# Scratch of the placed expert weights: from key pair, partition, token tile to partition, token tile, key pair

## The chip, the cores and the metric

One core of a Trainium2 chip runs the whole kernel. The metric is the device time of one execution in microseconds.

## What is computed

The kernel is one layer of a hybrid backbone for 1024 latent and 256 context tokens (10 tiles of 128, width 1024): modulated norm, an input projection, neighbourhood and context attention, a bidirectional gated scan, an output projection, and then PEER, a product-key layer of experts with one neuron each. The change is in PEER:

```
s = einsum('nhpd,pkd->nhpk', q, sub_keys)            # 8 heads, two halves, 128 keys
...                                                  # top 16 of each, top 16 of their sums
expert = (idx1 * N_KEYS + idx2)                      # 128 of 16384 experts for each token
g = softmax(best)                                    # a weight for each of them
act = gelu(einsum('cd,ced->ce', x_c, u[e_c]))
out = einsum('ce,ced->cd', g_c * act, v[e_c])
```

## The kernel before

Six of the ten token tiles fetch the rows of u and v that their tokens chose, with indirect DMAs that GpSimd issues. The first four tiles (512 tokens, "dense") go through all 16384 experts instead: 64 rounds of one key pair, 2 x 128 experts. A round computes gelu of the products of the tokens with u (two u tiles, `exp_a_ps`, L2573), multiplies it by the placed weights (L2838), which are 0 where a token did not choose the expert, and multiplies by v (`exp_o_ps`, L2600 and L2605). In the same rounds gathered tiles are worked off beside it: rounds 0 to 7 ("keys") fetch 10 or 14 key rows each, the later ones 8 key rows and two groups of four value rows, each row 128 x 4 KB.

**The placing stage** (`place_weights`) makes the placed weights of the dense tiles. For each tile there are 8 steps of 16 tokens, in four batches of 4 tokens. VectorE makes one-hots (L2110 to L2125), ScalarE scales them or makes a part of them (L2215 to L2229), TensorE multiplies them, and ScalarE copies the products into the grid (`placed`, L2237). There are two grids, tile t writes grid t % 2, so tile 2 waits at its first copy for the store of tile 0, tile 3 for that of tile 1. A grid holds 64 KB in each partition, in the order key pair r, token half h, key of the pair e, token n (for the last tile: half first). Partition a is the second key. Beside it, GpSimd fetches 24 key rows and the last 56 value rows of a context tile, in a ring of six rows, four rows a group; TensorE takes a group (`late_products`, L2151) in the middle of every second step, in program order, and GpSimd refills the rows only when the group is done.

The stores go to a scratch tensor in HBM. Sync issues tiles 0 to 2 whole (L2261) as each is placed, then the first half of tile 3's tokens (L2263), then of the second half the first two key pairs (L2265), while ScalarE's queue stores the other 62 pairs (L2253). Sync then waits for the stores of tiles 0 to 2, and the stage ends.

**The experts' stage** (`experts`). Sync's queue issues in each round the load of that round's placed weights into `g_raw` (L2488, after both products at L2838 of the round before), the v pair and two u tiles; in the late rounds in the order g, v (after TensorE's products of the round before), u, u (each after the u products that free it). VectorE needs `g_raw` at L2838. The load of round r, in the layout before, reads `scratch["g"][r]`, which is contiguous:

```
ROOM = {... "g": (N_KEYS // 2, P, DENSE_TILES, 2, 2, P // 2), ...}            # L2957
sp.dma_start(tile_target(t), tile_grid(t)).then_inc(stored[t % 2], 16)        # L2261
sp.dma_start(g_raw[:, :, :, :], scratch["g"][r].rearrange("a t h e n -> a (t h) e n"))  # L2488
```

So a store of a tile writes 128 x 64 runs of 1 KB (512 B for the halves of tile 3), and a load reads 128 runs of 4 KB.

Of the kernel before, what the change touches and what calls it, by code (L numbers as in the profile page):

```python
# [17 lines left out]
P = 128  # L18
D = 1024
KD = D // P  # L20
LATENT, CONTEXT = 1024, 256
T = LATENT + CONTEXT
TILES = T // P
LATENT_TILES = LATENT // P
DENSE_TILES = 4
# [12 lines left out]
N_KEYS = 128  # L38
# [1936 lines left out]
def place_weights(nc, io, keep, scratch, routes, ahead, edge):  # L1975
# [13 lines left out]
    with Scope(nc, "place") as s:  # L1989
# [35 lines left out]
        LAST_TILE = DENSE_TILES - 1  # L2025
        HALF_TOKENS = P // 2

        def tile_target(t):
            return scratch["g"].rearrange("r a t h e n -> a r t (h e n)")[:, :, t, :]

        def tile_grid(t):
            return grid[t % 2][:, :].rearrange("p (r x) -> p r x", x=2 * P)

        def half_target(h, lo, hi):
            return scratch["g"].rearrange("r a t h e n -> a r t h (e n)")[:, lo:hi, LAST_TILE, h, :]

        def half_grid(h, lo, hi):
            return grid[LAST_TILE % 2][:, :].rearrange("p (h r x) -> p h r x", h=2, x=P)[:, h, lo:hi, :]
# [137 lines left out]
        def _(act):  # L2176
# [64 lines left out]
            def body(t, m, before):  # L2241
# [9 lines left out]
            copy_batches(TOTAL - 1, (2, 3))  # L2251
            act.wait_ge(placed, DENSE_TILES * PER_TILE)
            nc.scalar.dma_start(half_target(1, FIRST_PAIRS, N_KEYS // 2), half_grid(1, FIRST_PAIRS, N_KEYS // 2))\  # L2253
              .then_inc(edge.g_rest, 16)

        @block.sync
        def _(sp):
            sp.dma_start(ahead.x[:, 0, :], scratch["h2"][0]).then_inc(edge.x_in[0], 16)
            for t in range(LAST_TILE):
                sp.wait_ge(placed, (t + 1) * PER_TILE)  # L2260
                sp.dma_start(tile_target(t), tile_grid(t)).then_inc(stored[t % 2], 16)  # L2261
            sp.wait_ge(placed, LAST_TILE * PER_TILE + PER_TILE // 2)
            sp.dma_start(half_target(0, 0, N_KEYS // 2), half_grid(0, 0, N_KEYS // 2)).then_inc(edge.g_half, 16)  # L2263
            sp.wait_ge(placed, DENSE_TILES * PER_TILE)
            sp.dma_start(half_target(1, 0, FIRST_PAIRS), half_grid(1, 0, FIRST_PAIRS)).then_inc(edge.g_first, 16)  # L2265
            sp.wait_ge(stored[0], 32)
            sp.wait_ge(stored[1], 16)


def experts(nc, io, keep, scratch, ahead, edge):  # L2270
# [21 lines left out]
    with Scope(nc, "exp") as s:  # L2292
# [13 lines left out]
        g_raw = s.sb("g_raw", [P, 2 * DENSE_TILES, 2, P // 2])  # L2306
        acc = keep["acc"]
        h2T = acc[:, :, :].rearrange("p t n -> p (t n)").rearrange("p (k n) -> p k n", k=KD)
# [35 lines left out]
        g_in = s.sem("g_in")  # L2344
# [36 lines left out]
        y_out = s.sem("y_out")  # L2381
        own_pool = s.sem("own_pool")
        block = s.block()
        v_pairs = io["v_rows"].rearrange("p (r e) n -> p r e n", e=PAIR)

        def f32(a):
# [43 lines left out]
        def at_least(r, n):  # L2430
            return not isinstance(r, int) or r >= n
# [37 lines left out]
        def _(sp):  # L2469
            def load_u(n, e):  # L2470
                if not has_key(n):
                    return
                sp.wait_ge(a_made, n + 1)
                sp.dma_start(u_in_lo[:, e, :, :], io["uT"][n]).then_inc(u_in[e], 16)

            def body(r, parity, mode, tile, _):
                if mode == "end":
                    load_rows()
                    return
                if tile == 0:  # L2480
                    sp.dma_start(xs[1], scratch["h2"][1]).then_inc(x_in[1], 16)
                def load_g():
                    if at_least(r, 1):
                        sp.wait_ge(weighted, 2 * r)
                    else:
                        sp.wait_ge(edge.g_half, 16)
                        sp.wait_ge(edge.g_first, 16)
                    sp.dma_start(g_raw[:, :, :, :], scratch["g"][r].rearrange("a t h e n -> a (t h) e n")).then_inc(g_in, 16)  # L2488

                if mode == "keys":  # L2490
                    if at_least(r, 1):
                        load_g()
                    load_u(2 * r + 2, 0)
                    load_u(2 * r + 3, 1)
                    if not at_least(r, 1):
                        load_g()
                    if at_least(r, 2):
                        sp.wait_ge(o_made, DENSE_TILES * (r - 1))
                    sp.dma_start(v_whole[parity][:, :, :], v_pairs[:, r, :, :]).then_inc(whole_in[parity], 16)
                else:  # L2500
                    load_g()
                    sp.wait_ge(o_made, DENSE_TILES * (r - 1))
                    sp.dma_start(v_raw[parity][:, :, :], v_pairs[:, r, :, :]).then_inc(v_in, 16)
                    for e in range(PAIR):
                        load_u(2 * r + 2 + e, e)
                if isinstance(r, int) and r == 1:
                    sp.wait_ge(edge.g_rest, 16)
                if tile is not None and tile >= 2:
                    store(tile - 2)
                if mode == "both" and tile is not None and tile + 1 < LATENT_GATHER:  # L2510
                    sp.wait_ge(dots, SLOTS * tile + RING)
                    sp.dma_start(xs[(tile + 1) % 2], scratch["h2"][tile + 1]).then_inc(x_in[(tile + 1) % 2], 16)

            def store(k):
                sp.wait_ge(out_ready, k + 2)
                sp.dma_start(scratch["ffn"][k + DENSE_TILES], out[:, :]).then_inc(out_stored, 16)

            def load_rows():
                sp.wait_ge(out_stored, 16 * LATENT_GATHER)
                sp.wait_ge(a_made, N_KEYS + 2)  # L2520
                sp.dma_start(gate_row[LATENT_COND], scratch["gate"][:, LATENT_COND, :]).then_inc(gate_in[LATENT_COND], 16)
                for t in STORED_TILES:
                    if t == STORED_TILES[-1]:
                        sp.wait_ge(dots, SLOTS * LATENT_GATHER + HALF_SLOTS + RING)
                    if t == LATENT_TILES:
                        sp.dma_start(gate_row[CONTEXT_COND], scratch["gate"][:, CONTEXT_COND, :])\
                          .then_inc(gate_in[CONTEXT_COND], 16)
                    sp.dma_start(ffn_row(t), scratch["ffn"][t]).then_inc(final_in[t], 16)
                    sp.dma_start(mixed_row(t), scratch["x1"][t]).then_inc(final_in[t], 16)
                    if t == STORED_TILES[0]:  # L2530
                        sp.dma_start(norm_w, io["norm_f"].partition_broadcast(P)).then_inc(norm_in, 16)
                for t in [SUMMED_TILE] + list(range(DENSE_TILES)):
                    sp.dma_start(mixed_row(t), scratch["x1"][t]).then_inc(final_in[t], 16)
# [420 lines left out]
            walk(dve, lambda r, parity, mode, tile, local: end(r) if mode == "end" else body(r, parity, mode, tile, local))  # L2954


ROOM = {"x1": (TILES, P, D), "h2T": (P, KD, DENSE_TILES * P), "g": (N_KEYS // 2, P, DENSE_TILES, 2, 2, P // 2),  # L2957
        "h2": (GATHER_TILES - CONTEXT_GATHER, P, D), "gate": (P, 2, D), "ffn": (TILES, P, D)}


def program(nc, io):
    scratch = {name: nc.dram_tensor(f"scratch_{name}", shape, FP32).ap() for name, shape in ROOM.items()}
    with Scope(nc, "keep") as s:
# [129 lines left out]
```

## Time and profile before

| what | value |
|---|---|
| median of 3 runs | 3399.52 us (3398.56 to 3399.75) |
| the profiled execution | 3391.75 us |
| its span, first to last instruction | 3389.2 us |
| TensorE, VectorE, GpSimd, ScalarE busy | 91%, 79%, 59%, 31% of the span |
| DMA | 1131.17 MB in 365083 packets, mean 334 GB/s |
| of it the gathers' queue (q0) | 221184 packets, 805.40 MB |
| of it Sync's queue (q1) | 135248 packets, 316.40 MB |
| of it ScalarE's queue (q10) | 8496 packets, 7.44 MB |
| placing stage, first to last copy into a grid | 1412.2 to 1613.7 us |
| rounds, first and last load at L2488 | 1635.4 and 3301.7 us |

Times in the trace count from the start of the span. A busy share is an average over stages; which wait comes last in a stage is read from windows, waits and timelines of that stage. In the counts of a queue every descriptor's move is a packet, and each gathered row adds a few packets of 4 bytes (the signals). The share of a queue is the time that its packets took over that of all 16 engines; packets overlap a little, so shares can add up to more than 100%.

### The profile page before, as it was taken

What the parts mean: (1) busy time and instruction counts of PE and PEld (TensorE: products, weight loads), DVE (VectorE), ACT (ScalarE), POOL (GpSimd) and SP (SyncE); (2) the same over time, 40 slices, a digit from 0 to 9 for tenths busy, and PEclk for the clock granted to TensorE, in tenths of its full rate; (3) what the DMA queues carried; (4) which work ended last, traced back from release to release, by engine and by line L of the source; (5) the groups of instructions that cost most, each with busy time, mean ns of one, the idle gap of its engine ahead of it and who ended that gap; (6) DMA issues with size and microseconds to landing.
All of it is one profiled execution on the core that took longest, in us unless ns stands there. A gap on an engine that the chain in (4) does not pass through costs nothing.

```text
span 3389.2 us, 46100 instructions
## 1 busy us (share of the span) xinstructions
PE 3081.4 (91%) x15031; PEld 2028.2 (60%) x15031; DVE 2663.5 (79%) x5959; ACT 1052.9 (31%) x1893; POOL 1983.3 (59%) x1674
## 2 busy tenths in 40 slices
PE   6879899789899998677699999999999999999996
PEld 4647344566455445366455677766777766677674
DVE  2327899688487999799699778887888888787888
ACT  4731244366111111488211222222222222222222
POOL 0000477444445555553588777787777777777771
PEclk9989999899899999899799999999999999999998
DMA  9422698665867888899999999999999999999997
GB/s 332 178 103 105 214 312 296 205 199 181 336 248 254 292 288 304 315 347 384 353 384 405 407 413 412 413 413 412 412 414 413 413 412 413 413 414 413 412 412 306
DMA packets 365083, 1131.17 MB, mean 334 GB/s; under 512 B 31944, under 2 KB 98760, under 8 KB 356608
## 3 DMA queue, kind: packets, MB, share of 16 engines
q0 software_dynamic: 221184, 805.40, 62.3%
q1 hardware_dynamic: 135248, 316.40, 24.5%
q10 hardware_dynamic: 8496, 7.44, 0.7%
q8 instruction: 80, 1.31, 0.1%
q14 instruction: 75, 0.61, 0.0%
HBM read 1075.93 MB, written 53.19 MB: 333 GB/s over the span
## 4 chain that ended last, share of the span: by engine, by line
PE 18%; DMA 12%; POOL 10%; issue 8%; DVE 3%; ACT 0%; POOLq 0%; SPq 0%; DVEq 0%; ACTq 0%
DMA exp_value_row<-in_v_rows,exp_v_id 11%; PE exp_a_ps L2573 8%; PE exp_o_ps L2600 5%; POOL exp_value_row L2729 5%; PE exp_v_ps L2557 3%; PE exp_o_ps L2605 2%; POOL edge_u_raw L2718 1%; POOL exp_more_row L2718 1%; POOL edge_row L2718 1%; POOL exp_value_row L2718 1%; DVE edge_u_raw L2783 1%; DMA exp_value_row<-in_u_rows,edge_id_and_dot 0%; DMA exp_final_row<-scratch_x 0%; DVE exp_u_lo L2747 0%; POOL exp_v_id L2700 0%
## 5 line engine op out<-in xcount | busy, mean ns | idle before, releaser
L423 POOL DMA_INDIRECT ahead_row<-in_u_rows,keep_tables x194 | 272.5, 1404 | 571.5 <-POOLq L102 356.3
L2729 POOL DMA_INDIRECT exp_value_row<-in_v_rows,exp_v_id x448 | 500.4, 1117 | 158.8 <-issue 134.7
L2573 PE MATMUL exp_a_ps<-exp_xT_hi,exp_u_hi 128*128 128x512 f32 x1024 | 410.8, 401 | 31.3 <-DVE exp_u_lo L2747 23.0
L2573 PE MATMUL exp_a_ps<-exp_xT_lo,exp_u_hi 128*128 128x512 f32 x1024 | 401.2, 392 | 0.0
L2573 PE MATMUL exp_a_ps<-exp_xT_hi,exp_u_lo 128*128 128x512 f32 x1024 | 400.5, 391 | 0.0
L2718 POOL DMA_INDIRECT edge_row<-in_u_rows,edge_id_and_dot x224 | 307.3, 1372 | 104.0 <-issue 48.4
L2656 ACT ACTIVATE exp_hidden<-exp_a_ps 128x512 f32<-128x512 f32 x128 | 76.6, 598 | 916.0 <-PE exp_a_ps L2573 916.0
L2864 DVE TENSOR_TENSOR keep_acc<-exp_o_ps,keep_acc 128x1024 f32<-128x1024 f32 x250 | 305.2, 1221 | 58.8 <-PE exp_o_ps L2600 52.5
L2600 PE MATMUL exp_o_ps<-exp_v_hi,exp_w_hi 128*128 128x512 f32 x896 | 287.3, 402 | 7.4 <-DVE keep_acc L2913 7.4
L2600 PE MATMUL exp_o_ps<-exp_v_lo,exp_w_hi 128*128 128x512 f32 x896 | 282.4, 396 | 0.0
L2600 PE MATMUL exp_o_ps<-exp_v_hi,exp_w_lo 128*128 128x512 f32 x896 | 280.5, 394 | 0.0
L2573 PEld LDWEIGHTS exp_a_ps<-exp_xT_hi,exp_u_hi 128*128 128x128 f32 x1024 | 193.3, 189 | 118.9 <-issue 48.0
L432 DVE CUSTOM_DVE_ANT_0 ahead_row<-ahead_row,ahead_x 128x1024 f32<-128x1024 f32 x194 | 231.0, 1219 | 25.8 <-DMA ahead_row<-in_u_rows,keep_tables 25.4
L2557 PE MATMUL exp_v_ps<-exp_value_row,exp_hot 128*32 128x512 f32 x1792 | 218.6, 600 | 29.1 <-DMA exp_value_row<-in_v_rows,exp_v_id 29.1
L1546 PE MATMUL queries_q_ps<-mix_featT,queries_slab 128*128 128x512 f32 (+1 forms) x640 | 230.3, 512 | 0.0
L495 POOL DMA_INDIRECT val_row<-in_v_rows,keep_tables x136 | 145.5, 1070 | 126.1 <-PE route_lat_h_ps L509 65.6
L2573 PEld LDWEIGHTS exp_a_ps<-exp_xT_hi,exp_u_lo 128*128 128x128 f32 x1024 | 193.3, 189 | 41.8
L2600 PEld LDWEIGHTS exp_o_ps<-exp_v_hi,exp_w_hi 128*128 128x128 f32 x896 | 164.3, 189 | 90.0 <-issue 45.3
L2573 PEld LDWEIGHTS exp_a_ps<-exp_xT_lo,exp_u_hi 128*128 128x128 f32 x1024 | 193.5, 189 | 39.9 <-issue 1.7
L2783 DVE CUSTOM_DVE_ANT_0 edge_row<-edge_row,keep_tables 128x1024 f32<-128x1024 f32 x128 | 155.9, 1218 | 56.3 <-DMA edge_row<-in_u_rows,edge_id_and_dot 56.3
L737 PE MATMUL proj_lat_ps<-mix_featT,heads_early_room 128*128 128x512 f32 x448 | 196.4, 596 | 1.8 <-ACTq L796 1.8
L2626 ACT ACTIVATE exp_u_hi<-exp_u_raw 128x1024 fp32r<-128x1024 f32 x126 | 132.6, 1053 | 195.9 <-DMA exp_u_raw<-in_uT 195.8
(451 smaller groups left out, 6375.4 us busy)
## 6 DMA issues: line engine op xcount, KB each, us to landing
exp_u_raw<-in_uT SPq DMA_DIRECT2D x126, 512.0 KB, 6.7
exp_v_raw<-in_v_rows SPq DMA_DIRECT2D x56, 1024.0 KB, 7.8
exp_g_raw<-scratch_g SPq DMA_DIRECT2D x64, 512.0 KB, 7.9
scratch_g<-place_grid SPq DMA_DIRECT2D x3, 8192.0 KB, 52.1
proj_ctx_mod_slab<-in_w_mod SPq DMA_DIRECT2D x8, 2048.0 KB, 13.3
heads_early_room<-in_w_in SPq DMA_DIRECT2D x10, 1024.0 KB, 12.5
mod_slab<-in_w_mod SPq DMA_DIRECT2D x4, 2048.0 KB, 20.3
queries_slab<-in_w_q SPq DMA_DIRECT2D x4, 2048.0 KB, 25.4
```

What stands on the lines that cost most here:

```text
L423: nc.gpsimd.indirect_dma_start(out=row, out_offset=None, in_=io["u_rows"], in_offset=bass.IndirectOffsetOnAxis(ap=ahead.keep["expert_id"]. ...
L432: nc.vector.tensor_tensor_reduce(out=row, in0=row, in1=ahead.x[:, n // SLOTS - ahead.first, :], scale=1.0, scalar=0.0, op0=ALU.mult, op1=A ...
L495: nc.gpsimd.indirect_dma_start(out=val.rows[slot][:, t, :], out_offset=None, in_=io["v_rows"].rearrange("a b n -> (a b) n"), in_offset=bas ...
L737: last = nc.tensor.matmul(ps[C * (ct % 2) + c][:, 0:width], early.slab(a, ct // 2)[:, k, ct % 2 * P:(ct % 2 + 1) * P], hT[:, k, g.at + at: ...
L1546: last = nc.tensor.matmul(q_ps[:, 0:width], slab[:, k, ct * P:(ct + 1) * P], h2T[:, k, at:at + width], start=(k == 0), stop=(k == KD - 1))
L2557: mm = nc.tensor.matmul(v_ps[QUAD * t:QUAD * (t + 1), half * SLAB:(half + 1) * SLAB], hot[:, i % 2, t, :], value_row[:, 4 * (i % 2) + t, h ...
L2573: mm = nc.tensor.matmul(a_ps[e][:, :], u[part][:, e, k, :], xT[xp][:, k, :], start=(k == 0 and part == 0 and xp == 0), stop=(k == KD - 1 a ...
L2600: mm = nc.tensor.matmul(o_ps[t % 2][:, c, :], w[1 - parity][part][:, e, t * P:(t + 1) * P], v[1 - parity][xp][:, e, c * SLAB:(c + 1) * SLA ...
L2718: nc.gpsimd.indirect_dma_start(out=row, out_offset=None, in_=io["u_rows"] if mode != "last" else io["v_rows"].rearrange("a b n -> (a b) n" ...
L2729: nc.gpsimd.indirect_dma_start(out=value_row[:, 4 * (j % 2) + t, :], out_offset=None, in_=io["v_rows"].rearrange("a b n -> (a b) n"), in_o ...
L2783: nc.vector.tensor_tensor_reduce(out=row, in0=row, in1=x, scale=1.0, scalar=0.0, op0=ALU.mult, op1=ALU.add, accum_out=dot[:, parity, j:j + ...
L2864: nc.vector.tensor_tensor(acc[:, t, :], o_ps[t % 2][:, :, :].rearrange("p c n -> p (c n)"), acc[:, t, :], ALU.add).then_inc(added, 1)
```

## The change

The scratch tensor is laid out by partition, token tile, key pair. The stores write to the same grid elements' new places: a partition's part of tiles 0 to 2 is 64 KB without a gap in HBM, as it is in the grid; the halves of tile 3 are runs of 512 B that now lie 1 KB apart instead of 512 KB. The load of a round reads four runs of 1 KB in each partition, 64 KB apart, and partitions lie 256 KB apart. The order of issues, the semaphores and every compute instruction stay as they are.

```diff
--- before.py
+++ after.py
@@ -2026,13 +2026,13 @@
         HALF_TOKENS = P // 2
 
         def tile_target(t):
-            return scratch["g"].rearrange("r a t h e n -> a r t (h e n)")[:, :, t, :]
+            return scratch["g"].rearrange("a t r h e n -> a t r (h e n)")[:, t, :, :]
 
         def tile_grid(t):
             return grid[t % 2][:, :].rearrange("p (r x) -> p r x", x=2 * P)
 
         def half_target(h, lo, hi):
-            return scratch["g"].rearrange("r a t h e n -> a r t h (e n)")[:, lo:hi, LAST_TILE, h, :]
+            return scratch["g"].rearrange("a t r h e n -> a t r h (e n)")[:, LAST_TILE, lo:hi, h, :]
 
         def half_grid(h, lo, hi):
             return grid[LAST_TILE % 2][:, :].rearrange("p (h r x) -> p h r x", h=2, x=P)[:, h, lo:hi, :]
@@ -2381,6 +2381,7 @@
         y_out = s.sem("y_out")
         own_pool = s.sem("own_pool")
         block = s.block()
+        by_round = scratch["g"].rearrange("a t r h e n -> a r t (h e n)")
         v_pairs = io["v_rows"].rearrange("p (r e) n -> p r e n", e=PAIR)
 
         def f32(a):
@@ -2485,7 +2486,7 @@
                     else:
                         sp.wait_ge(edge.g_half, 16)
                         sp.wait_ge(edge.g_first, 16)
-                    sp.dma_start(g_raw[:, :, :, :], scratch["g"][r].rearrange("a t h e n -> a (t h) e n")).then_inc(g_in, 16)
+                    sp.dma_start(g_raw[:, :, :, :].rearrange("a (t h) e n -> a t (h e n)", h=2), by_round[:, r, :, :]).then_inc(g_in, 16)
 
                 if mode == "keys":
                     if at_least(r, 1):
@@ -2954,7 +2955,7 @@
             walk(dve, lambda r, parity, mode, tile, local: end(r) if mode == "end" else body(r, parity, mode, tile, local))
 
 
-ROOM = {"x1": (TILES, P, D), "h2T": (P, KD, DENSE_TILES * P), "g": (N_KEYS // 2, P, DENSE_TILES, 2, 2, P // 2),
+ROOM = {"x1": (TILES, P, D), "h2T": (P, KD, DENSE_TILES * P), "g": (P, DENSE_TILES, N_KEYS // 2, 2, 2, P // 2),
         "h2": (GATHER_TILES - CONTEXT_GATHER, P, D), "gate": (P, 2, D), "ffn": (TILES, P, D)}
```

## Rows read from the trace of the kernel before

**Rows 1.** The page, its 40 slices: what the DMA engines moved, GB/s.
```profile
GB/s 332 178 103 105 214 312 296 205 199 181 336 248 254 292 288 304 315 347 384 353 384 405 407 413 412 413 413 412 412 414 413 413 412 413 413 414 413 412 412 306
```

**Rows 2.** Windows: us, busy (count) by engine, PEclk, DMA share, GB/s; placing and a late round.
```profile
1532.00:1542.00 10.00, 8.86 (x75) 7.08 (x73) 10.00 (x23) 9.13 (x27) 5.73 (x5) 1.00 1.05 406
2421.00:2448.00 27.00, 26.80 (x136) 18.97 (x132) 22.30 (x31) 6.58 (x9) 20.88 (x18) 1.00 1.03 413
```

**Rows 3.** Timeline of Sync's queue (start, us): the loads at L2488 of rounds 8 and 63.
```profile
1821.54 0.34 SPq L2488 DMA_DIRECT2D exp_g_raw<-scratch_g  x1
...
3301.65 0.33 SPq L2488 DMA_DIRECT2D exp_g_raw<-scratch_g  x1
```

**Rows 4.** Queue counts (packets, MB, share), 1589 to 1591 us: 1 KB packets alone.
```profile
q1 hardware_dynamic: 745, 0.76, 108.5%
```

**Rows 5.** Queue counts, 2802 to 2806 us: the gathers' 4 KB rows alone.
```profile
q0 software_dynamic: 451, 1.64, 102.2%
```

**Rows 6.** Queue counts, 1627 to 1631 us: 4 KB (q0) beside 512 B (q10).
```profile
q0 software_dynamic: 370, 1.32, 87.8%
q10 hardware_dynamic: 370, 0.19, 15.6%
```

**Rows 7.** Queue counts, 2808 to 2811 us: 8 KB (q1) beside 4 KB (q0).
```profile
q1 hardware_dynamic: 107, 0.88, 69.0%
q0 software_dynamic: 111, 0.40, 32.4%
```

**Rows 8.** Queue counts, 1593 to 1597 us: 16 KB (q10) beside 1 KB (q1).
```profile
q10 hardware_dynamic: 98, 1.61, 96.4%
q1 hardware_dynamic: 99, 0.10, 7.1%
```

**Rows 9.** DMA issues: count, KB each, median us from issue to landing.
```profile
exp_g_raw<-scratch_g SPq DMA_DIRECT2D x64, 512.0 KB, 7.9
scratch_g<-place_grid SPq DMA_DIRECT2D x3, 8192.0 KB, 52.1
```

**Rows 10.** Timeline of TensorE and VectorE after a store [idle before <-releaser].
```profile
1469.19 0.63 PE L2151 MATMUL place_v_ps<-edge_u_raw,keep_tables 128*32 128x512 f32 x2 [1.96 <-DMA keep_acc<-in_v_rows,keep_tables]
...
1519.91 0.91 PE L2151 MATMUL place_v_ps<-keep_acc,keep_tables 128*32 128x512 f32 x2 [2.15 <-DMA edge_u_raw<-in_v_rows,keep_tables]
...
1524.63 1.23 DVE L2115 TENSOR_TENSOR place_hot<-keep_iota,place_cols 128x1024 f32<-128x1024 f32 x1 [2.52 <-PE place_ps L2170]
```

**Rows 11.** L2261 (issue ns min/median/max, first and last start), and the issue at L2265.
```profile
L2261 SPq DMA_DIRECT2D scratch_g<-place_grid x3: 373/383/388, 1460.6 to 1563.1; - x3
...
1614.29 3.67 SPq L2265 DMA_DIRECT2D scratch_g<-place_grid  x1
```

**Rows 12.** Timeline of GpSimd: two value gathers around the first store.
```profile
1459.40 0.93 POOL L2066 DMA_INDIRECT keep_acc<-in_v_rows,keep_tables  x1 [0.30 <-issue]
1460.64 1.22 POOL L2066 DMA_INDIRECT keep_acc<-in_v_rows,keep_tables  x1 [0.31 <-issue]
```

**Rows 13.** Queue counts, first 1457 to 1462 us, then 1462 to 1464 us.
```profile
q0 software_dynamic: 171, 0.62, 41.8%
...
q0 software_dynamic: 102, 0.37, 61.2%
```

**Rows 14.** Waits, 1460 to 1584 us: VectorE behind TensorE (us, times, longest).
```profile
DVE place_hot L2115 <- PE place_ps L2170: 4.6, 5, 2.5
```

**Rows 15.** Timeline of VectorE: its first instruction of the experts' stage, round 0's first product.
```profile
1618.90 0.06 DVE L2743 MEMSET exp_eps<- 128x1 f32 x1 [7.50 <-PEq L102]
...
1644.16 0.69 DVE L2838 TENSOR_TENSOR exp_whole_w<-exp_hidden,exp_g_raw 128x512 f32<-128x512 f32 x1 [10.23 <-DMA exp_g_raw<-scratch_g]
```

**Rows 16.** Timeline of Sync's queue and VectorE: a late round's loads, and the use.
```profile
2791.92 0.33 SPq L2488 DMA_DIRECT2D exp_g_raw<-scratch_g  x1
2804.34 0.33 SPq L2503 DMA_DIRECT2D exp_v_raw<-in_v_rows  x1
...
2812.46 0.69 DVE L2838 TENSOR_TENSOR exp_hidden<-exp_hidden,exp_g_raw 128x512 f32<-128x512 f32 x1 [1.71 <-ACT exp_hidden L2656]
```

## The prediction

> **What bounds the kernel now.** I read the page first: how busy the engines are, and the line of DMA rates. TensorE is busy 91% of the span, but from the 22nd to the 39th of the 40 slices the DMA engines move 405 to 414 GB/s [rows 1]. The windows by stage [rows 2] say which of the two binds. In the placing stage VectorE is busy 10.00 us out of 10 and DMA moves about 400 GB/s; in a late round TensorE is busy 26.8 us of 27 and DMA 1.03 of its share. One late round moves 8 key rows and 8 value rows of 512 KB, two u tiles of 512 KB, a v pair of 1 MB and 512 KB of placed weights: 10.5 x 1.049 = 11.01 MB, which at 413 GB/s is 26.66 us. From the load of round 8 to that of round 63 there are (3301.65 - 1821.54) / 55 = 26.91 us each [rows 3]. So all but 0.25 us of a late round is the time of its bytes: the rounds are bound by DMA, the placing stage by VectorE, with DMA close behind.
>
> The change touches only descriptors, so the third thing to read is what one costs and how two queues share an engine, from short stretches of the queue counts. Alone, 745 packets of 1 KB pass in 2 us [rows 4]: 16 x 2 / 745 = 43.0 ns each on an engine. Alone, the gathers' 4 KB rows make 1.64 MB in 4 us, 400 of them [rows 5]: 160 ns. With two queues full the engines serve **one packet of each in turn, whatever the size**: 370 of 4 KB against 370 of 512 B [rows 6]; 107 of 8 KB against 111 of 4 KB [rows 7]; 98 of 16 KB against 99 of 1 KB, 427 GB/s together [rows 8]. From the last, a 16 KB packet costs 16 x 4 / 98 - 0.04 = 0.61 us. That is the key to this change. Packets of 4, 8 and 16 KB are each one partition's contiguous run, so a run is not cut on the way.
>
> **Part 1, the store of tiles 0 to 2 (L2261).** Now it is 128 x 64 runs of 1 KB and lands after 52.1 us [rows 9], while the gathers take most of the bandwidth: each of their turns is 4 KB, each of the store's 1 KB. After the change a partition's tile is one run of 64 KB on both sides, 128 descriptors, 8 to an engine. No row shows a packet over 16 KB; scaled from that one it takes 4 x 0.61 = 2.44 us, and with one 4 KB row between, 2.60 us a turn. The store then needs 8 x 2.60 = 20.8 us instead of 52, but in those 20.8 us an engine serves only 8 packets of gathers, the whole of a single gather (128 rows over 16 engines).
>
> Who waits for gathers there? TensorE, in program order, for the four late value rows of each group (L2151); behind that wait stand the placing products, ScalarE's copies and VectorE's one-hots, which can't run further ahead than their four buffers. The slack is nothing already: at each of the three stores TensorE came to its group and waited some 2 us for value rows (1.96 at the first, 2.15 at the second), and the second wait went through at once: VectorE's next one-hot began after 2.52 us of idleness [rows 10].
>
> The first store goes out at 1460.6, the last at 1563.1 [rows 11]; all three lie the same way to their groups. The two gathers that the next group still needs are issued around it, at 1459.40 and 1460.64 [rows 12]. The store's packets come some 2 us after its issue: from 1457 to 1462 only the gathers' queue has packets, 171 of them, and in the next 2 us it has 102 [rows 13]. So at 1462.5 some 196 packets have passed, 128 of the key gather ahead and 68 of the first value gather; 60 + 128 = 188 are still to come, 11.75 to an engine. Eight go inside the store, which ends at 1462.5 + 20.8 = 1483.3; the rest take 0.6 us, and I add 0.9 us for landing: 1484.8, against 1469.19 now [rows 10]. **The stall is 15.6 us**, three times: **+46.8 us**. VectorE was at its limit and can't make it up. Bounds: +7 us if 64 KB goes as pieces of 16 KB (turns of 0.77 us: 9 to 12 turns end 1 to 4 us late), 0 if as 4 KB, and +50 us if TensorE also runs 1 us each time at its lower clock after the idleness. I take 46.8, because the three sizes measured all hold their turn.
>
> What the faster store gives back: VectorE's idleness behind TensorE in the stage is 4.6 us in all from 1460 to 1584 us [rows 14], most of it at the three groups counted above; -1 us. The wait for a free grid at tiles 2 and 3 costs nothing now and goes.
>
> The Trainium skill (DMA: Bandwidth & Descriptors, Queues, rings and completion order) says that an engine drains a whole packet, typically 9 to 17 descriptors, from one ring before it switches. The trace does not show that: the counts above show one run to a turn; by that rule all 8 runs of an engine would go in one turn, no gather would pass, and the sum would be about 1.3 us higher for each store.
>
> **Part 2, the last tile.** Its halves stay runs of 512 B, as many as before. But the first half (4 MB) now queues behind tile 2's store: the issue of the first pairs at 1614.29 takes 3.67 us [rows 11], where that of a whole tile into an empty ring takes 0.38; the ring is still full. Sync must issue that before the stage's end, and VectorE enters the next stage after 7.50 us of waiting for it [rows 15]. With tile 2 gone in 21 us the ring is empty and the issue takes 0.4 us, as others do: **-3.3 us** on the path, since TensorE's first products hang on VectorE's first splits. Bounds: 0 and -3.7.
>
> **Part 3, the read of a round (L2488).** 128 runs of 4 KB become 512 of 1 KB; the DMA total of a saturated round grows by 8 x (4 x 43.0 - 160) = 96 ns on each engine. For 56 rounds (8 to 63) **+5.4 us**; in rounds 0 to 7, where a round has fewer bytes, TensorE covers it. The measured 1 KB packets are writes to HBM; a read could be dearer, which is a rival below. Latency: 32 turns beside the gathers instead of 8, that is 32 x (0.160 + 0.043) = 6.5 us instead of 8 x 0.32 = 2.6 us, so a load lands about 3.9 us later than its 7.9 us [rows 9]. In a late round it is issued at 2791.92 and used at 2812.46 [rows 16], 20.5 us later: covered. The v load behind it in the queue goes out at 2804.34 [rows 16], about when it lands: covered. If that cover were gone it would be 3.9 us a round. Only round 0 waits openly, 10.23 us [rows 15]; there the gathers are nearly drained, and the longer load costs **+0.8 us** (bounds 0 and 4).
>
> **The sum.** 46.8 - 1 - 3.3 + 5.4 + 0.8 = **+48.7 us**. The profiled execution took 3391.75 us (span 3389.2 us), which makes 3440.5 us; the median of the runs, 3399.52 us, is 7.8 us above it, and I put the change on the median: 3448.2 us, forecast **3448 us**. This case's own range is 3430 to 3462.
>
> **The rivals.** (a) *Long runs are cut, or the two dimensions aren't joined.* At 16 KB: 7 - 1 - 3.3 + 5.4 + 0.8 = +8.9, 3408 us; at 4 KB, +1.9, 3401 us; if runs stay 1 KB nothing of parts 1 and 2 happens: +6.2, 3406 us. For it: nothing over 16 KB was seen. Against: every contiguous run seen came as one packet.
> (b) *A slow read.* Runs of 1 KB whose starts lie 64 KB (tiles) and 256 KB (partitions) apart may fall on the same part of HBM. If they come at three quarters of the rate, the 1.3 us that 512 KB take alone (11.01 MB in 26.66 us) become 1.7: 56 x 0.4 = +22 us, 3470 us. Against: v is read today from rows 512 KB apart and reaches 8 KB packets at 425 GB/s together [rows 7]; the stores now write 1 KB runs 512 KB apart at 43.0 ns each [rows 4]. The Trainium skill (DMA: Bandwidth & Descriptors, Latency and other measured facts) gives this as HBM row pitch at large powers of two: 207 GB/s at 512 KiB, 164 at 2 MiB, 103 at 4 MiB. By its ladder a pitch of 256 KiB costs nothing; the trace of v agrees as far as 512 KB.
> (c) *Faster.* Short packets of weights leave the gathers' queue more turns, so value rows land earlier in a round, and the long runs hold no turn. Then rounds fall from 26.91 us to the floor of bytes, 26.66 + 0.10 = 26.76: -8 us; with -1 and -3.3 from the stage and +0.8, 3388 us. It decides if DMA has idle time inside rounds. Against: it moves 412 to 414 GB/s in each slice from the 24th to the 39th [rows 1], and a queue of its own taking long turns is what rows 6 to 8 show.
>
> **How the numbers follow.** A measurement can tell about 0.2% (7 us). Chances: forecast 0.68; (a) 0.14, of which half counts as within 0.2%; (b) 0.06; (c) 0.12, of which 0.02 falls within 0.2%. Faster 0.10, same 0.09, slower 0.81. The range reaches down to the cut runs, 3401, and up to the slow read, 3470: 3400 to 3470; left out are (c), tails of (a) and (b), and a stall of another size.
>
> **What would show it.** In the profile after: the three stores land in about 21 to 24 us; beside them one gather's packets to the store's 128; TensorE idle some 15 us before L2151 three times, VectorE behind it; the placing stage about 45 us longer; the issue at L2265 short; loads of weights landing near 12 us; late rounds 0.1 us longer at 411 GB/s. The forecast is wrong if gathers flow beside the stores (no wait over 5 us at L2151), or if the rounds change by more than 0.3 us.

## The result: 60.8 us slower

| | before | after |
|---|---|---|
| median of 4 runs each | 3399.28 us | 3460.11 us (3457.52 to 3464.01) |
| the profiled execution | 3391.75 us | 3462.18 us |
| its span | 3389.2 us | 3459.4 us |
| ratio of the times, 95% interval | | 1.0188 [1.0172, 1.0203] |

The forecast was 3448 us in a range of 3400 to 3470; the sign and the mechanism are those of the forecast, the size was 48.7 us for a measured 60.8. The two profiled executions lie 70.2 us apart in span, 9.4 more than the medians: that of before was 7.5 us under its median, that of after 2.1 us over its own. The span is split at five instructions of Sync's queue, taken from the two timelines:

| stretch | before | after | difference | forecast |
|---|---|---|---|---|
| start to the first store (nothing is changed there) | 1460.58 | 1464.79 | +4.2 | 0 |
| first store to the issue at L2265 | 153.71 | 205.89 | +52.2 | +45.8 |
| that to the first load of weights | 21.13 | 17.80 | -3.3 | -3.3 |
| loads of rounds 0 to 8 | 186.12 | 190.22 | +4.1 | +0.8 |
| loads of rounds 8 to 63 | 1480.11 | 1492.67 | +12.6 | +5.3 |
| last load to the end | 87.55 | 88.03 | +0.5 | +0.1 |

The first line moves by itself: in the runs below, which leave this stretch alone, the first store lies anywhere from 1459.5 to 1469.1 us. The other lines add up to 66.0 us, 5 more than the medians differ by, so the lines up to round 8 are good to some microseconds only: a run below with the stores of before (the read alone) has 158.06 us where this table has 153.71. Rounds 8 to 63 are steadier: two other runs with the loads of before took 1479.92 and 1480.16 us for them. Lines behind L2383 of the kernel have moved down by one (L2488 is L2489 now, L2838 is L2839).

The page of after, which answers to [rows 1]: the 23rd to the 39th slice, 407 to 414 GB/s before, now stand near 409, and the 18th to the 20th, 347, 384 and 353 GB/s before, have fallen to 311, 269 and 318.

```profile
GB/s 337 162 119 84 243 296 300 191 196 161 355 247 261 298 287 338 284 311 269 318 378 381 409 409 409 409 410 409 409 409 409 410 409 409 409 409 411 408 409 305
```

**How the queues shared the engines.** Queue counts of after beside the first store, in 16 us (packets, MB, share); this answers to [rows 8], with 64 KB in place of 16:

```profile
q1 hardware_dynamic: 99, 6.49, 96.8%
q0 software_dynamic: 96, 0.39, 6.3%
```

One run of 64 KB for one row of 4 KB, 99 to 96. Sync's queue moved 6.49 MB in that time, the gathers 0.39 MB. Nothing was cut: 6.49 MB in 99 packets are 65.5 KB each. A turn of both took 16 x 16 / 99 = 2.59 us on an engine, where the forecast had 2.60. The Trainium skill (DMA: Bandwidth & Descriptors, Queues, rings and completion order) has an engine drain a packet of typically 9 to 17 descriptors before it switches; by that the gathers would have had no turn within a store. The counts don't show it, at 64 KB any more than at 16. The three stores landed after 24.9 us in the median, for 52.1 before [rows 9].

**Who waited.** TensorE's timeline in after, as in [rows 10] (start us, us, line, tiles, [idle before <- releaser]), the three groups of value rows behind the three stores:

```profile
1490.22 1.07 PE L2151 MATMUL place_v_ps<-edge_u_raw,keep_tables 128*32 128x512 f32 x2 [18.78 <-DMA keep_acc<-in_v_rows,keep_tables]
...
1558.84 1.07 PE L2151 MATMUL place_v_ps<-keep_acc,keep_tables 128*32 128x512 f32 x2 [18.80 <-DMA edge_u_raw<-in_v_rows,keep_tables]
...
1627.57 3.64 PE L2151 MATMUL place_v_ps<-keep_acc,keep_tables 128*32 128x512 f32 x16 [19.08 <-DMA keep_acc<-in_v_rows,keep_tables]
```

TensorE came to the first group at 1490.22 - 18.78 = 1471.44, 6.65 us after the store's issue, just as before (1469.19 - 1.96 - 1460.58 = 6.65). The rows came 16.8 us later. Of before, [rows 10] show the first two groups; the third, and VectorE's one-hots behind the first and the third, are:

```profile
1472.27 1.23 DVE L2115 TENSOR_TENSOR place_hot<-keep_iota,place_cols 128x1024 f32<-128x1024 f32 x1 [0.69 <-PE place_ps L2170]
...
1571.42 1.95 PE L2151 MATMUL place_v_ps<-keep_acc,keep_tables 128*32 128x512 f32 x16 [1.69 <-DMA keep_acc<-in_v_rows,keep_tables]
...
1574.50 1.23 DVE L2115 TENSOR_TENSOR place_hot<-keep_iota,place_cols 128x1024 f32<-128x1024 f32 x1 [0.42 <-PE place_ps L2170]
```

VectorE's one-hots behind the three groups of after:

```profile
1495.34 1.23 DVE L2115 TENSOR_TENSOR place_hot<-keep_iota,place_cols 128x1024 f32<-128x1024 f32 x1 [19.55 <-PE place_ps L2170]
...
1563.79 1.23 DVE L2115 TENSOR_TENSOR place_hot<-keep_iota,place_cols 128x1024 f32<-128x1024 f32 x1 [19.40 <-PE place_ps L2170]
...
1632.34 1.22 DVE L2115 TENSOR_TENSOR place_hot<-keep_iota,place_cols 128x1024 f32<-128x1024 f32 x1 [19.50 <-PE place_ps L2170]
```

TensorE waited 16.8, 16.7 and 17.4 us longer than before, 50.9 us in all; VectorE, which bounds the stage, waited 18.9, 16.9 and 19.1 us longer, 54.8 us in all. GpSimd stands behind TensorE too; the waits of 1400 to 1720 us (us in total, times, longest), which answer to [rows 14]:

```profile
ACT place_grid L2237 <- PE place_ps L2170: 63.0, 12, 19.9
DVE place_hot L2115 <- PE place_ps L2170: 59.1, 4, 19.5
...
POOL keep_acc L2066 <- PE place_v_ps L2151: 39.4, 3, 19.5
PE place_v_ps L2151 <- DMA keep_acc<-in_v_rows,keep_tables: 39.3, 3, 19.1
```

The windows of after (PE, PEld, DVE, ACT, POOL busy, then granted clock, DMA share, GB/s) show the stall and what follows it:

```profile
1471.00:1490.00 19.00, 0.44 (x4) 0.25 (x3) 4.79 (x12) 4.35 (x12) 1.68 (x1) 0.58 0.96 397
1490.00:1495.00 5.00, 4.78 (x23) 1.95 (x24) 0.00 (x0) 0.00 (x0) 0.81 (x1) 0.55 0.54 220
1495.00:1500.00 5.00, 4.75 (x42) 4.56 (x41) 4.66 (x9) 3.51 (x10) 4.08 (x4) 1.00 0.70 199
1500.00:1515.00 15.00, 11.79 (x96) 9.51 (x95) 15.00 (x35) 13.51 (x39) 7.57 (x7) 1.00 0.73 253
```

In the first, DMA is 96% busy, and no engine for more than about a quarter. Then the store is done, GpSimd has only just been allowed to refill the ring, and DMA runs at 220, 199 and 253 GB/s where [rows 2] show about 400: the bandwidth that the gathers missed is not made up, since they can't be fetched ahead. The granted clock was 0.55, 0.52 and 0.59 in the 5 us in which TensorE took up work after its three waits, mostly the lower of its two levels (1.2 GHz of 2.4). From TensorE's start on the group to VectorE's next one-hot it took 5.12, 4.95 and 4.77 us. Before, it took 3.08 us at the first and the third group, where the granted clock was 1.00, and 4.72 us at the second (1524.63 - 1519.91, [rows 10]), where it was 0.66 from 1519 to 1524 us. So the low clock accounts for 2.0, 0.2 and 1.7 us, 4.0 in all, and that is the difference between VectorE's 54.8 us and TensorE's 50.9.

**The end of the stage**, Sync's timeline and VectorE's, for [rows 11, 15]:

```profile
1464.79 137.38 SPq L2261 DMA_DIRECT2D scratch_g<-place_grid  x3
1645.91 0.38 SPq L2263 DMA_DIRECT2D scratch_g<-place_grid  x1
1670.68 0.38 SPq L2265 DMA_DIRECT2D scratch_g<-place_grid  x1
...
1672.03 0.06 DVE L2744 MEMSET exp_eps<- 128x1 f32 x1 [4.23 <-PEq L102]
...
1697.95 0.69 DVE L2839 TENSOR_TENSOR exp_whole_w<-exp_hidden,exp_g_raw 128x512 f32<-128x512 f32 x1 [11.01 <-DMA exp_g_raw<-scratch_g]
```

The issue at L2265 takes 0.38 us for 3.67, VectorE's wait for the stage's end 4.23 for 7.50, round 0's wait for its weights 11.01 for 10.23.

**The rounds**, for [rows 3, 9] and the second of [rows 2]: loads of rounds 8 and 63, the landing of loads, a late window.

```profile
1878.70 0.58 SPq L2489 DMA_DIRECT2D exp_g_raw<-scratch_g  x1
...
3371.37 0.57 SPq L2489 DMA_DIRECT2D exp_g_raw<-scratch_g  x1
...
exp_g_raw<-scratch_g SPq DMA_DIRECT2D x64, 512.0 KB, 11.5
...
2500.00:2527.00 27.00, 26.39 (x130) 18.92 (x130) 21.68 (x32) 6.62 (x10) 18.91 (x19) 1.00 1.03 409
```

From round 8 to round 63 there are 1492.67 / 55 = 27.139 us each, for 26.911 before. DMA is as saturated as it was (1.03), and moves less.

### The profile page after: what moved, and what is told of

It is laid out like the page before. It is cut to its first block, busy times and chain, and to the rows that moved or that the text cites. A ratio compares the mean times of both kernels' runs of the same rounds, so it can differ in the third digit from the quotient of the medians.

```text
span 3459.4 us, 46100 instructions
## 1 busy us (share of the span) xinstructions
PE 3094.3 (89%) x15031; PEld 2031.0 (59%) x15031; DVE 2663.7 (77%) x5959; ACT 1051.3 (30%) x1893; POOL 1968.2 (57%) x1674
## 4 chain that ended last, share of the span: by engine, by line
PE 20%; DMA 14%; issue 6%; POOL 6%; DVE 4%; ACT 0%; POOLq 0%; SPq 0%; DVEq 0%; ACTq 0%
DMA exp_value_row<-in_v_rows,exp_v_id 12%; PE exp_a_ps L2574 9%; PE exp_o_ps L2601 6%; PE exp_v_ps L2558 4%; POOL exp_value_row L2730 2%; PE exp_o_ps L2606 2%; POOL exp_more_row L2719 1%; POOL edge_u_raw L2719 1%; POOL exp_value_row L2719 1%; POOL edge_row L2719 1%; DVE edge_u_raw L2784 1%; DVE exp_v_lo L2748 0%; DMA exp_final_row<-scratch_x 0%; DMA exp_value_row<-in_u_rows,edge_id_and_dot 0%; ACT exp_hidden L2657 0%
## 5 line engine op out<-in xcount | busy, mean ns | idle before, releaser
L2730 POOL DMA_INDIRECT exp_value_row<-in_v_rows,exp_v_id x448 | 486.7, 1086 | 184.6 <-issue 135.7
L2574 PE MATMUL exp_a_ps<-exp_xT_hi,exp_u_hi 128*128 128x512 f32 x1024 | 411.0, 401 | 28.7 <-DVE exp_u_lo L2748 23.7
L2719 POOL DMA_INDIRECT edge_row<-in_u_rows,edge_id_and_dot x224 | 292.2, 1304 | 103.4 <-issue 46.0
L2601 PEld LDWEIGHTS exp_o_ps<-exp_v_hi,exp_w_hi 128*128 128x128 f32 x896 | 164.4, 189 | 90.8 <-issue 48.7
## 6 DMA issues: line engine op xcount, KB each, us to landing
exp_g_raw<-scratch_g SPq DMA_DIRECT2D x64, 512.0 KB, 11.5
mod_slab<-in_w_mod SPq DMA_DIRECT2D x4, 2048.0 KB, 20.2
```

The lines of the kernel that those rows point to most:

```text
L2574: mm = nc.tensor.matmul(a_ps[e][:, :], u[part][:, e, k, :], xT[xp][:, k, :], start=(k == 0 and part == 0 and xp == 0), stop=(k == KD - 1 a ...
L2601: mm = nc.tensor.matmul(o_ps[t % 2][:, c, :], w[1 - parity][part][:, e, t * P:(t + 1) * P], v[1 - parity][xp][:, e, c * SLAB:(c + 1) * SLA ...
L2719: nc.gpsimd.indirect_dma_start(out=row, out_offset=None, in_=io["u_rows"] if mode != "last" else io["v_rows"].rearrange("a b n -> (a b) n" ...
L2730: nc.gpsimd.indirect_dma_start(out=value_row[:, 4 * (j % 2) + t, :], out_offset=None, in_=io["v_rows"].rearrange("a b n -> (a b) n"), in_o ...
```

## The experiments

Times of a run are medians; its ratio is to the kernel before, run between on the same chip. "Stage" is the stretch from the first store to the issue of the first pairs' store (153.71 us before, 205.89 after), in one profiled execution of each kernel.

**Stores in smaller runs.** If the stall hangs on the length of a run, shorter runs must take it away. The first two keep the layout of after and cut the run; the waits for the stores then count the pieces (not shown).

```diff
-                sp.dma_start(tile_target(t), tile_grid(t)).then_inc(stored[t % 2], 16)
+                for c in range(0, N_KEYS // 2, 4):      # 16 for the second
+                    sp.dma_start(tile_target(t)[:, c:c + 4, :], tile_grid(t)[:, c:c + 4, :]).then_inc(stored[t % 2], 16)
```

In 4 KB runs, 16 transfers a tile. Expected:

> The changed kernel, with each of the three tile stores issued as 16 transfers of four key pairs: runs of 4 KB in place of 64 KB, the same bytes to the same places. Turn theory (queues are served one packet of each in turn, so the size of the run decides what the gathers get): a turn falls from 2.6 us to 0.32, the 12 turns that the next value group needs take 3.8 us instead of 24; TensorE's waits for value rows in the placing stage come back from 56.7 us to 6 to 11 us, and the stage from the first store to the issue at L2265 from 205.9 us to 154 to 158. What stays is the dearer load of a round (+16 us) and the empty ring at the end (-3.3): 3412 to 3418 us. Rival (a store of 8 MB in a short time stalls the gathers whatever its runs, as it takes the bandwidth until it has landed): the waits stay near 19 us each, 3455 to 3460 us.

Measured: 3425.79 us, ratio 1.0085 [1.0068, 1.0102], stage 173.13 us, rounds 27.128. In 16 KB runs, 4 transfers a tile. Expected:

> The changed kernel, with each tile store issued as four transfers of 16 key pairs, runs of 16 KB. Turn theory: a turn is 0.61 + 0.16 = 0.77 us, the 12 turns take 9.2 us where 1 KB packets took 2.4: each of the three groups comes 3 to 7 us later than before, the waits of TensorE for value rows come to 15 to 27 us in sum, and the kernel to 3422 to 3434 us. Rival (bandwidth): as with 4 KB and 64 KB, 3455 to 3460 us, no order by size.

Measured: 3445.49 us, 1.0139 [1.0122, 1.0156], stage 189.12 us, rounds 27.161. So shorter runs do take the stall away step by step, but both times are above what was expected (3412 to 3418 and 3422 to 3434 us). The stage is 19.4 and 35.4 us longer than before, where my bounds for these sizes came to 0 and +7. The waits of the first, 1400 to 1690 us, are many and short, where after had three long ones:

```profile
PE place_v_ps L2151 <- DMA keep_acc<-in_v_rows,keep_tables: 21.8, 7, 5.3
PE place_v_ps L2151 <- DMA edge_u_raw<-in_v_rows,keep_tables: 5.4, 2, 3.0
```

The queue counts point to why. Beside the first store, 1477 to 1487 us, of before:

```profile
q0 software_dynamic: 714, 2.59, 63.4%
q1 hardware_dynamic: 1418, 1.45, 40.9%
```

The same of the kernel with 4 KB runs:

```profile
q1 hardware_dynamic: 671, 2.43, 60.1%
q0 software_dynamic: 487, 1.75, 42.7%
```

With 16 KB runs:

```profile
q1 hardware_dynamic: 237, 3.36, 80.3%
q0 software_dynamic: 229, 0.84, 20.6%
```

The gathers get 259, 175 and 84 GB/s in these 10 us, in after 24 (0.39 MB in 16 us). What they need can be judged by what they took between two stores of before, 1461 to 1512 us:

```profile
q0 software_dynamic: 3177, 11.57, 56.9%
q1 hardware_dynamic: 8202, 8.38, 46.8%
```

That is 227 GB/s, beside a store that takes the whole 51 us. What they miss under a faster store they would have to get after it, but the ring of six rows doesn't let them run ahead, and TensorE waits instead. With 4 KB runs the gathers' queue didn't even use all its turns: 1.75 MB are some 430 rows, to 671 packets of the store. My bounds had counted only how late the first group's rows come, not the rate of all that follow. This is a reading of counts; the paced stores below put it to the test.

**Runs of 1 KB in the new layout.** The same edit with pieces of one pair, 64 transfers a tile: the runs of before, at the addresses of after. Expected:

> The changed kernel, with each tile store issued as 64 transfers of one key pair: runs of 1 KB as before the change, to the new places, 256 KB apart by partition. It is the layout alone, without the long runs. Turn theory: gathers get 0.16 of each 0.20 us again, so TensorE's waits for value rows in the placing stage return to some 6 to 15 us and the stage from the first store to the issue of the first pairs to 154 to 160 us (153.7 before, 173.1 with 4 KB, 189.1 with 16, 205.9 with 64); the dearer load stays, rounds 27.13 us: 3408 to 3416 us. Rival (the new places in HBM are slower to write, and the size of the run only stood beside it): the stage stays at 170 us or more, 3425 us or more.

Measured: 3418.29 us, 1.0071 [1.0056, 1.0086]; the stage is 153.82 us, that of before. So, within the few microseconds by which executions differ, the layout costs the stage nothing and the length of the run all. But the time is 2 us above what I expected, and the timelines show where, in a term that I had not priced: Sync's, then VectorE's.

```profile
1569.93 42.90 SPq L2262 DMA_DIRECT2D scratch_g<-place_grid  x64
1612.87 0.44 SPq L2264 DMA_DIRECT2D scratch_g<-place_grid  x1
1619.18 11.00 SPq L2266 DMA_DIRECT2D scratch_g<-place_grid  x1
...
1631.13 0.06 DVE L2745 MEMSET exp_eps<- 128x1 f32 x1 [14.83 <-PEq L102]
```

The 64 issues of tile 2 take 42.9 us (that the room in the ring sets their pace is inferred); the store of the half, which had been placed by the 112th batch, goes out only behind them, and the issue of the first pairs then takes 11.00 us. VectorE waits 14.8 us for the stage's end, for 7.5 before; the load of round 0 comes 28.57 us behind that issue, for 21.13 before: +7.4 us.

**No gathers to starve.** The last 50 of the 56 late value rows are left out, and with them that part of the context tile's result; the products read the six rows that are there. Nothing else is changed, once in before and once in after.

```diff
-                    if i >= 4 * LATE_GROUPS:
+                    if i >= LATE_RING:
                         return
...
-                    pe.wait_ge(edge.late_in[i % LATE_RING], 16 * (i // LATE_RING) + 16)
+                    pe.wait_ge(edge.late_in[i % LATE_RING], 16)
```

Expected of before and of after:

> The kernel before, with only the first 6 of the 56 late value rows of the placing stage gathered, and all 14 groups of products made from those six (50 gathers of 512 KB are left out, all compute stays). It gives the stage without the gathers. Turn theory: TensorE waits for no value row, VectorE is the limit, and the stage from the first store to the issue of the first pairs falls from 153.7 to 147 to 152 us. Rival (the gathers don't matter): it stays at 153 to 155.

> The changed kernel with the same 50 gathers left out, the stores in runs of 64 KB. Turn theory: with nobody waiting for gathers the long runs cost nothing; the stage is within 3 us of that of the kernel before with the same gathers left out, some 55 us less than the 205.9 of the changed kernel. Rival (the store stops the stage itself, by the grids or the reads of SBUF beside ScalarE's writes): the stage stays 20 us or more above the other.

Measured, one execution each: 3391.54 us with a stage of 149.04, and 3400.21 us with a stage of 148.91. Of the waits of after without the rows (1400 to 1690 us) this is left at L2151:

```profile
PE place_v_ps L2151 <- DMA keep_acc<-in_v_rows,keep_tables: 2.0, 1, 2.0
DVE place_hot L2115 <- PE place_ps L2170: 1.6, 3, 1.1
```

The 64 KB runs are still there and cost the stage nothing. So, to within a few microseconds (one execution each), all of its 52 us goes by way of the value rows; neither VectorE's nor ScalarE's access to the grid, nor the wait for a free grid has a part in it that shows. The 8.7 us that the time still grows is the read: rounds 8 to 63 take 27.110 us each for 26.908, 11.1 us more in all, rounds 0 to 7 take 4.5 us more, less 6.6 us by which the first stretch differs between the two executions.

**The read alone.** Before's layout, with each round's 512 KB fetched in two transfers of 1 KB runs from a contiguous 512 KB: the count of packets of after, without its distances (VectorE's wait for a load then counts both; not shown).

```diff
-                    sp.dma_start(g_raw[:, :, :, :], scratch["g"][r].rearrange("a t h e n -> a (t h) e n")).then_inc(g_in, 16)
+                    for odd in range(2):
+                        sp.dma_start(g_raw[:, :, :, :].rearrange("a (t h) e n -> a t (h e n)", h=2)[:, odd::2, :],
+                                     scratch["g"][r].rearrange("a t h e n -> a t (h e n)")[:, odd::2, :]).then_inc(g_in, 16)
```

Expected:

> The kernel before, layout and stores unchanged, with the load of a round's placed weights issued as two transfers, each of every second tile's 1 KB: 512 packets of 1 KB whose starts lie 2 KB apart within a partition and 4 KB between partitions, in place of 128 of 4 KB. Count theory (the rounds got dearer by the number of packets): late rounds take 27.14 us each from load to load as in the changed kernel (26.91 before), DMA 409 GB/s, +12 to +17 us: 3411 to 3416 us. Pitch theory (they got dearer because runs lie 64 and 256 KB apart): rounds stay within 0.1 us of 26.91, +5 us at most: 3399 to 3404 us.

Measured: 3411.68 us, 1.0043 [1.0028, 1.0058], rounds 8 to 63 at 27.124 us and 409 GB/s. With no distance between runs a round grows by 0.213 us of the 0.228 of after. The other way round, after with 4 KB of padding behind each partition (the runs are then taken from a view of the unpadded part):

```diff
-ROOM = {..., "g": (P, DENSE_TILES, N_KEYS // 2, 2, 2, P // 2),
+ROOM = {..., "g": (P, DENSE_TILES * N_KEYS // 2 * 2 * P + 1024),
```

> The changed kernel, with 4 KB of padding behind each partition's part of the scratch, so that partitions lie 260 KB apart in place of 256. Count theory: nothing moves, late rounds 27.14 us, 3457 to 3464 us. Pitch theory: late rounds return to about 27.0 us or less, 3448 us or less.

Measured: 3459.08 us, 1.0179 [1.0162, 1.0196], stage 206.07 us, rounds 27.144 us. Nothing moves. The Trainium skill (DMA: Bandwidth & Descriptors, Latency and other measured facts) gives 207 GB/s at a row pitch of 512 KiB, falling to 103 at 4 MiB, and the full rate again at 4 MiB with 4 KiB of padding; its list doesn't reach down to this kernel's 256 KB between partitions, and there the two runs show no loss to cure. What is left is the number of packets.

**The full ring.** Did the 3.3 us at L2265 lie on the path? Before, with the first pairs' store issued from ScalarE's queue, ahead of that of the other 62:

```diff
-            sp.dma_start(half_target(1, 0, FIRST_PAIRS), half_grid(1, 0, FIRST_PAIRS)).then_inc(edge.g_first, 16)
...
+            nc.scalar.dma_start(half_target(1, 0, FIRST_PAIRS), half_grid(1, 0, FIRST_PAIRS)).then_inc(edge.g_first, 16)
             nc.scalar.dma_start(half_target(1, FIRST_PAIRS, N_KEYS // 2), half_grid(1, FIRST_PAIRS, N_KEYS // 2))\
```

> The kernel before, with the store of the last half's first two key pairs issued from ScalarE's queue, ahead of the other 62 pairs, in place of Sync's. Ring theory (Sync's issue takes 3.67 us at the stage's end because its ring is full with the first half, and the next stage waits for it): from the last copy's end to the first load of placed weights of round 0 the time falls by about 3 us, and the kernel to 3393 to 3397 us where the one before has 3397 to 3399. Rival (the issue waits for something that both queues share, or the next stage waits for another): no difference beyond 1 us.

Measured: 3396.48 us, 1.0013 [1.0002, 1.0024]: no gain. VectorE's wait for the stage's end does fall, to 5.48 us from 7.50, but ScalarE now issues two stores (0.41 and 1.28 us) ahead of its part of the new stage, and the move brings 1.5 us in the trace (20.2 us for 21.8 from the last copy into the grid to the first load) that the time doesn't show. Nor are the 3.3 us fixed in the stores of before. The run of the read alone has the same stores and the same placing stage, and shows:

```profile
1592.53 1.30 SPq L2263 DMA_DIRECT2D scratch_g<-place_grid  x1
1619.72 0.37 SPq L2265 DMA_DIRECT2D scratch_g<-place_grid  x1
```

The first half's issue takes 1.30 us there for 10.47 before, that of the first pairs 0.37 for 3.67. Yet from the first store to the first load it took 175.45 us, for 174.84 before: with the ring free the stretch was no shorter. So it is not shown that the 3.3 us that after gains at this place are worth anything in the time.

**Paced stores.** If the missing rate is the cause, and not the length of one turn, the same runs spread over more time should cost less. Sync waits for further batches before each piece (16 KB runs: 4 pieces, 7 batches apart for tiles 0 and 1; tile 2's must be gone by the half, so 5 apart; 4 KB: 16 pieces, 7/4 and 1 apart).

```diff
+                    later = 7 * c // 1 if t < 2 else 5 * c // 1
+                    sp.wait_ge(placed, (t + 1) * PER_TILE + later)
```

> The store in 4 KB runs lengthened the stage (first store to the issue at L2265) by 19 us, in 16 KB runs by 35 us. Two theories of that. (A) What counts is how long one run holds an engine: then it does not matter when the pieces go out, each 4 KB run still makes a gather's row wait, and the stage stays at about 173 us (3426 us in all). (B) What counts is the share of the bandwidth that the store takes while it lasts: 8.4 MB in about 35 us leave the gathers 165 to 210 GB/s where they need some 225; spread over the time that they took before (tiles 0 and 1: 16 pieces over 26 of the 32 batches of the next tile, about 42 us, 200 GB/s) they cost next to nothing. Tile 2's pieces can only be spread over half a tile (26 us), so one of the three stalls of about 6.5 us stays. Then the stage is 158 to 164 us, the time 3409 to 3417 us. Rounds at 27.13 us by both.

> The same with 16 KB runs in 4 pieces, each 7 batches (11 us) behind the last for tiles 0 and 1, 5 batches for tile 2. (A) length of a run: the stage stays near 189 us, 3445 us in all. (B) share over time: a 2 MB piece shuts the gathers out for about 5 us and then leaves them 6 us alone; six rows of ring cover some of that but not all, so 1 to 3 us for each piece of tiles 0 and 1 at most, mostly less: stage 158 to 172 us, 3410 to 3426 us.

This batch ran on a chip where before took 3412.67 us, so times compare only with that. Measured: in 4 KB runs 3425.96 us, 1.0040 [1.0026, 1.0054], stage 166.68; in 16 KB runs 3436.39 us, 1.0062 [1.0040, 1.0084], stage 168.80. The queue counts of the second, 1477 to 1487 us, between two of its pieces:

```profile
q0 software_dynamic: 704, 2.54, 69.5%
q1 hardware_dynamic: 17, 0.02, 0.5%
```

The gathers have their 254 GB/s there; from 1461 to 1512 us, pieces included, they have 9.94 MB, 195 GB/s.

If the length of a turn alone decided, the stages would have stayed near 189 and 173 us. The 16 KB runs show clearly that it doesn't: of the 35.4 us that they cost unpaced 15.1 are left. Of the 19.4 of the 4 KB runs 13.0 are left, a gain of 6.5 us that is not far above the spread of single executions. The times say more: against the before of the same chip the loss falls from 48.4 to 23.7 us with 16 KB and from 28.7 to 13.3 with 4 KB, and the intervals of paced and unpaced don't overlap. As differences these are what theory (B) expected, so it holds. But for 4 KB the time leaves nothing for the stage: the dearer read alone costs 1.0043. The stage of before was not traced on this chip, so how much of the 13.0 and 15.1 us is loss is open. Open, too, is why rounds 8 to 63 took 27.190 and 27.307 us here, for an expected 27.13; the excess lies in rounds 8 to 12, 148 us for 137 to 142 in the other runs. No version with all its gathers is faster than before.

## Why the prediction was right, and where its terms were off

- **Turns of one run each, uncut** held: 99 runs of 64 KB to 96 rows. So rival (a) falls at its first condition.
- **The stall, +46.8 us** (part 1): right in place, number and kind, too small. TensorE waited 50.9 us longer, for 3 x 15.6; the low clock adds 4.0, for the 3 us in the bound that I didn't take. The 1 us that a faster store was to give back was 2.4: VectorE's other waits behind TensorE in this stretch fell from 3.0 to 0.7 us. 50.9 + 4.0 - 2.4 = 52.5, for 52.2 measured and 45.8 forecast.
- **Its lower bounds, +7 us for 16 KB and 0 for 4 KB**, are the step that failed: the runs give +35.4 and +19.4 us. I worked out when the next group's rows come and took the gathers' queue as caught up from then on. But it needs 227 GB/s all the time, in a stage that [rows 2] show at about 400, and its six rows of ring leave little to catch up with: the store's share is paid for as long as it lasts. The paced stores bear that out; how the rest of the loss divides does not come out of them. Rival (a) at 16 KB would have been some 3445 us, not 3408. For 64 KB the same omission did little harm, in my reading because a store there shuts the queue for its whole length and the first group's delay is nearly all of the loss.
- **The ring at L2265, -3.3 us** (part 2): the trace shows -3.3 in the issue, in VectorE's wait and in the stretch. But neither moving the issue nor the execution in which the ring was free of itself (175.45 us from first store to first load, for 174.84) shows it in the time. That the number agrees is in part luck.
- **The read, +5.4 us for rounds 8 to 63** (part 3): right kind, mis-sized. It was 12.6 us over 55 rounds. An engine carries 8 runs of 4 KB a round, now 32 of 1 KB; (8 x 160 + 228) / 32 = 47 ns a run if all of the growth is DMA time, for the 43.0 that I took from writes. Four nanoseconds on a packet double the term, since it is a small difference of two large ones. The 43.0 were also measured alone, and the 47 beside gathers; which of the two, direction or company, makes the difference was not taken apart. In rounds 0 to 7 I counted nothing but round 0's +0.8, which came. The other 3.3 us lie in rounds 6 and 7, 52.6 us for 49.0, but the two other runs with the rounds of before took 51.5 and 51.6 there, so most of this is no effect of the change.
- **The slow read of rival (b)**: its price of 0.4 us a round was not reached (0.23), and its cause, distances in HBM, is excluded by the contiguous read and by the padding, both within 0.02 us of after.
- **Rival (c), faster**, fell on the stall and on rounds that grew: whatever turns the short packets of weights left to the gathers, the rounds got no shorter.
- The landing of a load at 11.5 us, 3.6 later for 3.9 forecast, was covered in late rounds as argued: behind round 0 the trace shows no wait of VectorE for `g_raw`.

What the median shows is 60.8 us: 70.2 us between the two traces less the 9.4 by which these two executions lie apart from their medians.

## What to carry to other kernels

In this kernel one contiguous run was one turn of a DMA engine, so long runs in one queue took bandwidth from the queue beside it: the gathers had 259 GB/s beside runs of 1 KB, 175 beside 4 KB, 84 beside 16 KB and 24 beside 64 KB. Before a background store is made "efficient", look for who fetches beside it, how far ahead that ring reaches, and whether DMA has room to catch up; if either is short, the short runs may have been what kept the other queue fed. And a layout has two sides: here 3 stores were made long at the price of 64 loads made short.

Bound a disturbance by the rate over its whole length, not by the delay of the first thing that it meets. Where the cost is a difference between packet sizes, take the price of a packet in the direction and the company of the transfer. And before a difference between two traces is given a cause, look at how far two executions of the same stretch lie apart.

## What was not expected of the hardware

- A run of 64 KB passes as one packet, and so took 96.8% of the engines' time (1470 to 1486 us) while the gathers' queue had nearly as many turns, 96 packets to 99.
- Runs of 1 KB cost about 47 ns when read from HBM beside gathers, for 43.0 ns written alone ([rows 4]); the contiguous read gives the same to 0.5 ns. Both are estimates, from the growth of a round.
- Many small transfers can hold the engine that issues them: the 64 issues of a tile took Sync 42.9 us where one transfer of the same 8192 runs took 0.37, and held up the one behind them.
- TensorE came back from its 19 us waits at a granted clock of 0.52 to 0.59, which made the three stalls 2.0, 0.2 and 1.7 us longer for VectorE.
